# A mixing phase whose early stage is split in two, with new task orders, four banks for the streams' states, block tables built across partitions, and residual rows kept in SBUF

## The reference, cut to what matters

```python
h = rmsnorm(x, ln1)
proj = h @ w_in                                   # 3080 columns
out_a = rglru(conv(proj[:512])) * gelu(proj[512:1024])
q, k, v = silu(conv(proj[1024:2560]));  z, beta, g = ...
# gated DeltaNet, 4 heads of 128: a scan over blocks of tokens
L = strict_lower(kb @ k.T * decay);  T = inv(I + L)
v_new = T @ (v*beta) - (T @ (kb*exp(gc))) @ S
o = (q*exp(gc)) @ S + (q @ k.T * decay) @ v_new
S = S*exp(g_last) + (k*exp(g_last-gc)).T @ v_new  # one S per head, per stream
x2 = x + concat(out_a, rmsnorm(o)*silu(z)) @ w_out
h2 = rmsnorm(x2, ln2)
grp, top-2 experts of the group, weights = router(h2)      # 32 experts
y[expert, slot] = (silu(h2 @ w1[e]) * (h2 @ w3[e])) @ w2[e]
out = rmsnorm(x2 + w_a*y[a] + w_b*y[b], final_g)
```

## Time and profile before

| | us |
|---|---|
| time, median of 3 runs (4146.07 to 4170.18) | 4149.03 |
| time of the profiled execution | 4149.71 |
| span of that execution in its profile | 4148.0 |
| PE busy, share of the span | 3463.8, 84% |
| DVE busy | 1822.0, 44% |
| ACT busy | 1314.6, 32% |
| POOL busy | 812.7, 20% |

### The profile page before, as it was taken

How to read it: one execution, slowest core, us unless ns; L and a number is a source line. 1 busy time by engine, 2 the same in 40 slices (tenths; PEclk the granted TensorE clock), 3 DMA queues, 4 the chain that set the end, 5 groups by cost and what they waited for, 6 DMA issues and landing times. The chain is left out here.

```text
span 4148.0 us, 60697 instructions
## 1 busy us (share of the span) xinstructions
PE 3463.8 (84%) x17484; PEld 2069.8 (50%) x17485; DVE 1822.0 (44%) x4823; ACT 1314.6 (32%) x2593; POOL 812.7 (20%) x1018
## 2 busy tenths in 40 slices
PE   7999999999975688888888877739999999999910
PEld 3444444444455666666666655624444444444400
DVE  6555456445544456556555555441111111111157
ACT  6455445545451233333323323201111111111122
POOL 0000000000001334434343433211111111111145
PEclk9999999999986799999999989859999999999965
DMA  4311111111013443443434333123445555553279
GB/s 144 102 49 48 51 66 38 53 51 53 33 39 123 131 121 116 127 120 114 130 99 129 96 98 103 50 108 143 182 182 200 186 187 207 197 188 121 86 309 379
DMA packets 334866, 514.03 MB, mean 124 GB/s; under 512 B 79874, under 2 KB 228834, under 8 KB 325986
## 3 DMA queue, kind: packets, MB, share of 16 engines
q1 hardware_dynamic: 251538, 279.19, 21.2%
q10 hardware_dynamic: 54288, 146.56, 9.0%
q0 software_dynamic: 28864, 86.09, 5.9%
HBM read 341.49 MB, written 170.26 MB: 123 GB/s over the span
## 5 line engine op out<-in xcount | busy, mean ns | idle before, releaser
L1745 PE MATMUL ebank<-w,rowsT 128*128 x1568 | 699.9, 600 | 32.6 <-SPq L1695 29.3
L298 PE MATMUL pP<-h_hi,w_hi 128*128 128x512 f16 (+1 forms) x1728 | 624.3, 365 | 31.4 <-DVE h_lo L480 16.8
L298 PE MATMUL pP<-h_lo,w_hi 128*128 128x512 f16 (+1 forms) x1728 | 624.3, 365 | 0.0
L298 PE MATMUL pP<-h_hi,w_lo 128*128 128x512 f16 (+1 forms) x1728 | 624.1, 365 | 0.0
L1745 PEld LDWEIGHTS ebank<-w,rowsT 128*128 128x128 f32 x1568 | 299.8, 192 | 418.5 <-issue 418.5
L1763 PE MATMUL ebank<-w,guT 128*128 x784 | 353.4, 593 | 2.6 <-ACT guT L1784 2.6
L1812 DVE TENSOR_TENSOR gu<-ebank,sil 128x256 f32<-128x256 f32 x98 | 41.6, 425 | 692.5 <-ACT sil L1780 692.5
L511 DVE SCALAR_TENSOR_TENSOR cv<-win,cols_sb,cv 128x512 f32<-128x512 f32 (+1 forms) x432 | 305.4, 707 | 35.1 <-issue 3.6
L1780 ACT ACTIVATE sil<-ebank 128x256 f32<-128x256 f32 x98 | 37.7, 385 | 814.8 <-PE ebank L1745 814.8
L298 PEld LDWEIGHTS pP<-h_hi,w_hi 128*128 128x128 f16 x1728 | 172.1, 100 | 220.6 <-issue 30.6
L298 PEld LDWEIGHTS pP<-h_lo,w_hi 128*128 128x128 f16 x1728 | 172.1, 100 | 187.2 <-issue 12.8
(11 more groups left out here) (308 smaller groups left out, 6237.1 us busy)
## 6 DMA issues: line engine op xcount, KB each, us to landing
w<-in_w SPq DMA_DIRECT2D x32, 2048.0 KB, 8.9
y<-yb ACTq DMA_DIRECT2D x98, 512.0 KB
ft<-mixin SPq DMA_DIRECT2D x33, 1280.0 KB, 7.1
mixin<-qo ACTq DMA_DIRECT2D x128, 256.0 KB, 2.0
w<-in_w SPq DMA_DIRECT2D x32, 1024.0 KB, 12.1
xt<-in_x SPq DMA_DIRECT2D x33, 512.0 KB, 5.1
kz<-mixin SPq DMA_DIRECT2D x33, 512.0 KB, 6.8
xr<-in_x SPq DMA_DIRECT2D x33, 512.0 KB, 5.3
```

Of the source, the lines that this page charges most:

```text
L298: ins = nc.tensor.matmul(pP[n % NPB][:, 0:N], w[:, k, c0:c0 + P], h[:, k, 0:N], start=(k + i == 0), stop=(k == KD - 1 and i == 2))
L1745: ins = nc.tensor.matmul((M0, M1)[p][:, :], xT[p][:, k, :], w13[:, bass.ds(s, 1), k * 512:(k + 1) * 512].rearrange("p a n -> p (a n)"), st ...
```

## The change

- **Mixing's early stage** becomes two: E (`gt`, `sq`, `stat`, `sse`, `ex`, `rr`, `fsc`) works on tile i+9, F (`gs`, `dec`, `DT`, `KK`, `G`, `QK`, `AT`, `ATm`) on i+8. In the prologue `stat` writes to bank YE, later to FB behind the previous tile's `QK`. `stat` computes 32 columns in a product and not 128. `sq` is ScalarE's first task of an iteration.
- **Task orders** are new on every engine: `x2` before `X`; `xn` before `vd`; GpSimd does `r2` right behind `eT`. The scatter is a stage Q one iteration later, in three pieces: `sct0` first of all, `sct1` behind `rr`, the wait for landing (`scd`) last.
- **SyncE** issues `early_load` between the stores of G and of AT, for a tile two ahead, so that it is there one iteration before its `sq`.
- **w_out** is split piece by piece, one in each of the first eight iterations. Setup waits for constants move to their first users.
- **The streams' states** use four banks and four mask buffers; ScalarE makes the masks.
- **Routing** is no phase of its own: the tables are computed with the blocks on partitions at the end of mixing (32 elements per operation), and turned into rows by two products on TensorE; the destinations are computed in three pieces at the start of the experts' phase, where the first weights are now loaded too.
- **Residual rows**: in the experts' phase SyncE also loads x2 of 28 tiles into SBUF (112 KB per partition), one after each expert's weights; the other five are loaded at the start of combining. Combining has no load of its own per tile any more.

```diff
 MIX = """
-Y.KS.pe Y.QS.pe Y.X.dve R.x2.dve Y.o1.act R.st.act X.eT.pool X.B16.pool X.eZ.pool R.r2.pool
-X.kt.pe X.vt.pe X.sc.dve X.ktc.act F.gs.dve F.sq.act
-Y.N.pe Y.vd.dve Y.vh.act X.vs.act R.xn.dve
-F.stat.pe F.sse.dve F.ex.act F.rr.pool X.B32.pool
-Y.dS.pe Y.AV.pe Y.S.dve
-R.hT0.pe R.hT1.pe R.hc0.dve R.hc1.dve Y.o.dve R.h2.pool
-X.W16.pe X.I16.dve F.dec.pe F.DT.act
-R.lg.pe F.fsc.dve R.r0.dve Y.so.act Y.ro.pool
-X.T16.pe X.T16c.act F.KK.pe F.G.dve X.B64.pool
-Y.outA0.pe X.Z16.pe X.Z16c.act R.r1.dve R.sh.act R.rx.act
+Q.sct0.pool X.eT.pool E.sq.act R.x2.dve Y.KS.pe Y.QS.pe Y.X.dve R.st.act Y.o1.act R.r2.pool X.B16.pool X.eZ.pool
+X.kt.pe X.vt.pe X.sc.dve E.gt.dve F.gs.dve X.ktc.act R.xn.dve
+Y.N.pe Y.vd.dve Y.vh.act X.vs.act
+E.stat.pe E.sse.dve E.ex.act E.rr.pool Q.sct1.pool R.h2.pool
+Y.dS.pe Y.AV.pe Y.o.dve Y.so.act Y.ro.pool
+R.hT0.pe R.hT1.pe R.hc0.dve R.hc1.dve
+X.W16.pe X.I16.dve Y.S.dve F.dec.pe F.DT.act E.fsc.dve
+R.lg.pe R.r0.dve X.T16.pe X.T16c.act X.B32.pool R.r1.dve
+F.KK.pe F.G.dve X.B64.pool
+Y.outA0.pe X.Z16.pe X.Z16c.act R.sh.act R.rx.act
 X.W32.pe X.I32.dve Y.outA1.pe Y.on.dve
-X.T32.pe X.T32c.act F.QK.pe F.AT.dve Y.oT.pe F.ATm.pool
+X.T32.pe X.T32c.act F.QK.pe F.AT.dve Y.oT.pe F.ATm.pool Q.scd.pool
...
-Y.outB0.pe Y.outB1.pe R.rk.pe V.v.dve R.off.dve R.sct.pool
+Y.outB0.pe Y.outB1.pe R.rk.pe V.v.dve R.off.dve
...
-                tiles_ = {st: tile_at(i, four, n) for st, n in (("F", LEAD), ("X", 1), ("Y", 0), ("R", -1))}
+                tiles_ = {st: tile_at(i, four, n) for st, n in (("E", LEAD + 1), ("F", LEAD), ("X", 1), ("Y", 0), ("R", -1), ("Q", -2))}
...
+                if after_first and four is None and 0 <= i + LEAD + 1 < KD:
+                    after_first(i + LEAD + 1)
...
                 if f is not None:
-                    early_store(f[0])
+                    G_store(f[0])
+                    if nf is not None:
+                        early_load(nf[0], nf[1])
+                    AT_store(f[0])
...
                 if n == "stat":
-                    pe.wait_ge(*at("AT", t, 1))
+                    if prologue(t):
+                        pe.wait_ge(*at("sse", t, 1))
+                        pe.wait_ge(*at("ex", t, 1))
+                    else:
+                        pe.wait_ge(*at("AT", t, 2))
+                    bank = flat(YE if prologue(t) else FB)
                     pe.wait_ge(*at("sq", t))
                     for c in range(2 * H):
-                        nc.tensor.matmul(flat(FB)[:, c:c + P], sqb[:, c, :], mat("ones"), start=True, stop=True)
+                        nc.tensor.matmul(bank[:, c:c + SW], sqb[:, c, :], mat("ones")[:, 0:SW], start=True, stop=True)
...
                 elif n == "dec":
-                    pe.wait_ge(*at("sse", t))
-                    pe.wait_ge(*at("ex", t))
+                    if stream or prologue(t + 1):
+                        pe.wait_ge(*at("AT", t, 1))
+                    else:
+                        pe.wait_ge(*at("sse", t, -1))
+                        pe.wait_ge(*at("ex", t, -1))
+                    pe.wait_ge(*at("gs", t))
...
                         for b in range(SB):
                             pe.wait_ge(vm_ready, b + 1)
+                            if b >= 4:
+                                pe.wait_ge(stream_S, b - 3)
                             for h in range(H):
-                                ins = nc.tensor.matmul(YC[:, h, :], ktok[p][:, h, :], vm[:, h, :], start=True, stop=True)
+                                ins = nc.tensor.matmul(turn_bank[b % 4][:, h, :], ktok[p][:, h, :], turn_vm[b % 4][:, h, :],
+                                                       start=True, stop=True)
                             ins.then_inc(stream_mm, 1)
-                            pe.wait_ge(stream_S, b + 1)
...
+            def routing():
+                v, part = nc.vector, col("part")
...
+                v.tensor_tensor_scan(end[:, :], start[:, :], nb[:, :], 0.0, ALU.mult, ALU.add)
+                v.tensor_scalar(past[:, :], end[:, :], part, None, ALU.is_le)
...
+                v.reduce_sum(route[:, 0:1], past[:, :], AX.X)
...
+                v.tensor_tensor(route[:, 1:2], route[:, 1:2], valid[:, :], ALU.mult).then_inc(route_columns, 1)
+                v.tensor_copy(tabs["end"][:, :], end[0:1, :])
+                dve.wait_ge(route_rows, 1)
+                v.tensor_copy(tabs["expert"][:, :], flat(YA)[0:1, 0:NB])
...
+            for p in range(2):
+                load_expert(sp, T, weights, p, p)
...
                     load_expert(sp, T, weights, pair * 2 + (2 + p), p)
+                    if keep:
+                        sp.dma_start(kept[0][:, bass.ds(pair * 2 + p, 1), :].rearrange("p a n -> p (a n)"),
+                                     T["x2"][bass.ts(pair * 2 + p, P), :]).then_inc(kept[1], 16)
...
+            def destinations():
+                iota, n = cols[:, COLS["iota"][0]:COLS["iota"][1]], 22
+                hot = yb[0][:, 0:n * NE].rearrange("p (t e) -> p t e", e=NE)
+                for c in range(0, 2 * NT, n):
...
+            destinations()
             program("dve", dve, step)
...
-                sp.dma_start(xx[p][:, :], T["x2"][bass.ts(t, P), :]).then_inc(x_in[p], 16)
+            for t in range(KEPT, NT):
+                sp.dma_start(late[:, t - KEPT, :], T["x2"][bass.ts(t, P), :]).then_inc(late_in, 16)
```

More of the change, by code:

```diff
@@ L37 @@
 FE = 256
+KEPT = NE - 4
 EPS = 1e-6
@@ L702, in mix_phase @@
         tid = sb("tid", [P, 1], I32)
+        cnt = sb("cnt", [P, NE], I32)
+        nb = sb("nb", [P, NE])
+        end = sb("end", [P, NE])
+        past = sb("past", [P, NE])
+        valid = sb("valid", [P, 1])
+        before = sb("before", [P, 1])
+        route = sb("route", [P, 2])
         FB, XA, XB, YA, YB, YC, YD, YE = [
@@ L761, in mix_phase, with prologue @@
         last = NT - 1
-        first_loop = 1
+        first_loop = 2
         loops = (last - 1 - LEAD - first_loop + 1) // BATCH
+        def prologue(t):
+            return isinstance(t, int) and t < LEAD
         def every(engine, iteration):
-            for i in range(-LEAD, first_loop):
+            for i in range(-LEAD - 1, first_loop):
                 iteration(i, None)
@@ L1281, in f_step @@
                     ins.then_inc(*did(n))
+                elif n == "gs":
+                    dve.wait_ge(*at("dec", t, 1))
+                    for h in range(H):
+                        ins = nc.vector.tensor_scalar(gs[:, h, :], mat("after_s" if stream else "after"),
+                                                      gt[p][:, H + h:H + h + 1], None, ALU.mult)
+                    ins.then_inc(*did(n))
                 elif n == "sse":
@@ L1634, in experts_phase @@
-def experts_phase(nc, T, const, tabs, weights):
+def experts_phase(nc, T, const, cols, eid, rank, start, dest, tabs, weights, kept):
     NT, NB = tiles(), blocks()
@@ L1836, in combine_phase @@
         yr = [[sb(f"yr{s}_{k}", [P, D]) for k in range(2)] for s in range(NR)]
-        xx = [sb(f"xx{s}", [P, D]) for s in range(NR)]
+        late = sb("late", [P, NT - KEPT, D])
         yo = [sb(f"yo{s}", [P, D]) for s in range(NS)]
@@ L1847, in combine_phase @@
         eps_set = sem("eps_set")
-        x_in = [sem(f"x2_in{s}") for s in range(NR)]
+        late_in = sem("late_in")
         y_in = [sem(f"y_in{s}") for s in range(NR)]
@@ L1992, in follow, with ahead @@
                 out(t, p)
-            with dve.Fori(0, NT // NR - 1) as four:
+            def ahead(t, p):
+                dve.wait_ge(y_in[p], both_fetched(t, p))
+                rows(t + NR, p)
+                follow(t, p)
+            whole = KEPT // NR - 1
+            with dve.Fori(0, whole) as four:
                 for p in range(NR):
-                    dve.wait_ge(y_in[p], both_fetched(four * NR + p, p))
-                    rows(four * NR + NR + p, p)
-                    follow(four * NR + p, p)
+                    ahead(four * NR + p, p)
+            for t in range(whole * NR, NT - NR - 1):
+                ahead(t, t % NR)
             rows(NT - 1, 0)
```

297 lines of the change are left out of this document (139 added, 158 removed).

## The result

The changed kernel takes 4057.05 us (median; the kernel before beside it 4158.74): a ratio of 0.9754, 95% interval 0.9709 to 0.9798. The forecast was 3902, the range began at 3855 and ended at 3985: the sign was right, the size was not. The medians differ by 101.7 us.

What follows compares the result with a forecast made beforehand. TensorE was taken to bound the experts, and a chain starting with GpSimd's queue the prompt tiles. Tiles 180, prologue 18, states 16, routing 25, residual rows 0 and combining 8 sum to 247 off 4149.7: 3902 us, range 3855 to 3985.

Steps and rivals of the forecast that it cites:

- Squares first: Prompt tiles: squares of q and k one tile ahead end TensorE's wait for them; 65 us gained, bounds 45 and 65.
- Scatter behind, `r2` forward: Prompt tiles: GpSimd's earlier `r2` brings `xn` early; 80 us back, 10 paid at `dS`, net 70, bounds 35 and 90.
- Narrow products: Full prompt tiles: passes with 32 columns instead of 128 start closer together; 25 us gained, bounds 0 and 32.
- Clock: Prompt tiles: with idle stretches gone, TensorE's granted clock partly comes back; 20 us gained, bounds 0 and 40.
- Prologue: Start of mixing: with E a tile ahead the scalars leave the chain between G's; 18 us gained, bounds 0 and 30.
- Streams' states: Eight state updates: with four banks the longest step decides; 14 us off plus 2, together 16, bounds 10 and 20.
- Routing: Between mixing and experts: tables hidden inside GpSimd's scatter wait, first expert product earlier; 25 us gained, bounds 18 and 28.
- Residual rows: Experts' phase: the 28 extra loads behind each expert's weights cost nothing; 0 us, bounds 0 and -6.
- combining: Combining: with a quarter fewer bytes, DVE's 4.65 us binds all 32 distances; 8 us gained, bounds 4 and 12.
- the stages hardly overlap more: Rival, prompt tiles: a chain through `vd` and `dS` replaces T's wait, clock stays 0.95; 3982; 0.28 with the VectorE rival.
- The one on VectorE: Rival, prompt tiles: DVE becomes the bound, 36.5 us a tile and not 33.9; 3985; 0.28 with the overlap rival.
- The one that was to end slower: Rival, full tiles: q and k load late and block ScalarE, 4200 us and more; chance 0.03.

Runs made afterwards that it cites:

- experiment 11: Changed kernel with `vd` ahead of `xn` on VectorE, but GpSimd's old order (both scatters, T, B16, Z, then `r2`): 4067.86 us, ratio 0.9789 to the kernel before.
- experiment 1: Changed kernel with `vd` ahead of `xn` in VectorE's task order: 4004.55 us, ratio 0.9625 to the kernel before.
- experiment 4: Changed kernel with the squares' and gates' products 128 columns wide again instead of 32: 4031.4 us, ratio 0.9694 to the kernel before.
- experiment 5: Kernel before the change with only the squares' and gates' products cut from 128 to 32 columns: 4195.71 us, ratio 1.0085 to the kernel before.
- experiment 6: Changed kernel with, in the prologue alone, the load of the tile two ahead issued before G's nine stores: 4045.92 us, ratio 0.9738 to the kernel before.
- experiment 7: Changed kernel with 128-column squares' products and a task order of its own for the prologue: 4022.28 us, ratio 0.9662 to the kernel before.
- experiment 3: Changed kernel with stage F ahead of stage E on every engine in the prologue: 4046.9 us, ratio 0.9729 to the kernel before.
- experiment 10: Changed kernel with `vd` ahead of `xn`, 128-column squares' products, the prologue's own order, and `xn` on ScalarE behind `vh`: 3964.82 us, ratio 0.9521 to the kernel before.

## Why the prediction was right and wrong

The time came out above the range because two steps failed, in the tiles (84.7 us for 180) and in the prologue (-36.7 for +18). In the tiles the step that failed is the overlap at the norm: `vd` behind `xn` was to cost `dS` 10 us and cost 62 more than before. In the prologue it is the path: the scalars did not leave the chain, and G's came 20.7 us apart for the 10.5 forecast. Two terms had the wrong sign besides, the narrow products and, in the full tiles, the clock.

*Squares first.* The wait went as forecast, 64.9 us to nothing. The time did not: the 25 tiles that have squares got 42.0 us shorter by all the edits together, so part of what was saved here was paid again at `dS` and in the clock. In the prologue the same step turned into the wait of 7.7 us a tile ahead of L952.

*Scatter behind, `r2` forward: net 70, bounds 35 and 90.* The step named its own risk, "`vd` stands behind `xn` on DVE now and `dS` waits for it", and priced it at 10 us; it cost 62. Two links in front of `xn` were laid out wrongly: T was given its blocks at once (it waited 73.8 us for them, SyncE's load coming after G's stores and five other transfers), and `xn` the 0.76 us that it took when GpSimd was quiet (1.75 here). The first half, GpSimd's order, is worth 63 us by experiment 11. The second, VectorE's, costs 53 by experiment 1. The second ate most of the first; what was left of 70 shows in the seven tiles without squares (42.7 us) and hardly in the full ones.

*Narrow products: 25, bounds 0 and 32.* The row was misread. The 0.07 us a pass of the earlier trace rows is the distance of starts within four passes that follow a product of 512 columns. The weight loads of the same four passes, in the same stretch of the kernel before, tell more:

```profile
1936.70 0.41 PEld L1089 LDWEIGHTS bank<-OO,const 128*128 128x128 f32 x2
1937.03 0.30 PEld L1090 LDWEIGHTS bank<-OO,const 128*128 128x128 f32 x2
1937.17 0.18 PEld L1069 LDWEIGHTS bank<-w_out_hi,mx_hi 128*128 128x128 f16 x1
```

The four loads take 0.47 us until the next one starts, 0.117 each: the first began beside the long product ahead, and that alone let the passes come closer. Sixteen in a row have nothing to hide behind and take just this, 0.117 with 32 columns, and 0.122 with 128 (experiment 4). The Trainium skill, "TensorE: Matmul & The Clock Gate", section "Back-to-back issue gap", adds that weight loads raise the distance above its floor; that was the half of its rule to go by, and for these passes it left next to nothing. (By that floor the term would be 57 us, as an estimate, 22 passes of 0.103 us less in 25 tiles, and not some 50.) The low bound said it, "weight loads could bind", and a bound below zero was missing: by the clock the edit costs 25 us in the changed kernel (ratio 0.9754 against 0.9694, experiment 4) and 35 to 39 in the one before (experiment 5).

*Clock: 20.* It went the other way in the full tiles, 0.95 to 0.93 (TensorE busy 7.5 us longer), and in the prologue, 0.66 to 0.53; in the seven tiles without stage F it came back as forecast, 0.88 to 0.95 (8.4 us less). What was argued, that less idle time brings it back, holds there and by experiment 1 (0.96; 1.00 in the tiles without stage F). In the full tiles of the changed kernel the wait at `dS` kept it down, 0.95 even with wide products (experiment 4), and the narrow products took the rest.

*Prologue: 18, bounds 0 and 30.* The failed step is "with E a tile ahead in its own bank the scalars leave the chain". They did not, because an order within each engine's queue, not a bank, holds them: `stat` of the tile ahead stands before `dec`, and it waits for a load that is issued behind nine stores. That is the low bound's own word, "SP's nine stores", with no price below zero. Of the 36.7 us 2.3 are the later start of mixing, and 4.2 the extra iteration, forecast 4 (from the first load to the first G 23.9 us against 19.7, with G's first start at 1275.07 and 1268.52). The other 30.2 are the loop from the first G to the first KS: 9.4 of them by the clock (gone in experiment 4), the rest by its order (experiments 6 and 7). Experiments 3 and 7 show what the sum left out besides: once `stat` is out of the way, `gs` stands on VectorE behind the w_out piece and the inversion's half, which were priced as work and not as links. And `dec` at full clock, as in the earlier trace rows (1.13 us), is not "at the low level, which holds here": that level held in part of the prologue.

*Streams' states: 16.* Right, 20.0. Updates now follow each other on VectorE without a gap, 32 in one row:

```profile
2635.41 8.36 DVE L1442 SCALAR_TENSOR_TENSOR S_s<-S_s,exS,bank 128x128 f32<-128x128 f32 x32 [2.13 <-PE bank L1069]
```

*Routing: 25, bounds 18 and 28.* 15.3. The tables are hidden behind the scatter as laid out; the first up-product then waits for the list and the gather one after the other (26.5 us of idle TensorE before the first transposes), which the sum had at 12 us from the end of mixing and which take 22. They now run beside two experts' weights on the same DMA engines; before, the weights were loaded under VectorE's tables. GpSimd's gather behind its wait for the list, before and after:

```profile
2791.20 1.02 POOL L1716 DMA_INDIRECT rows<-h,idx  x1 [2.57 <-DMA idx<-table]
```

```profile
2702.89 1.01 POOL L1728 DMA_INDIRECT rows<-h,idx  x1 [7.19 <-DMA idx<-table]
```

From there to the first transposes it took 4.6 us before and 9.6 after. Together the list and the gather take 9.7 us longer beside the weights, and 9.7 is what the term lacks. No run moved the weights, so the cause is read from these two traces alone.

*Residual rows: 0, bounds 0 and -6; combining: 8.* Right within the bounds, 3.6 lost and 8.5 gained; the sums of two tiles are 4.61 us apart (the second sums, 3902.9 to 4050.5 in 32 steps), forecast 4.65.

Of the rivals, "the stages hardly overlap more" came nearest: its chain through `vd` and `dS` is the one found, and the clock did not rise (0.93 over the 32 tiles). It was put at 3982 because it was summed with a prologue that gains 18. The one on VectorE had the other half of the mechanism, `xn` and `vd` in a row beside GpSimd's B16, and 36.5 us a tile (36.8 measured); but it is the order on VectorE and not its load, 24.3 us of 38.1 in a full tile, since swapping two tasks took the wait away (experiment 1). The one that was to end slower named the late load of q and k, but in the full tiles, where it is harmless; in the prologue, where the same load closes a loop, it was not looked for.

What stays open: why full tiles stay at 36.2 to 36.6 us where TensorE has 32 us of work. The largest waits left are WI and `lg`, then KS and the load of `ft`, and experiment 10 says only that 1.9 us less work on VectorE does not end them. Open too is why the narrower products lower the clock.

## What to carry to other kernels

When a producer is moved forward on an in-order queue, price what it now stands in front of: `xn` was early at last, and its own wait became that of everything behind it. When a task is moved to one tile ahead, walk once round the loop in the stretch where nothing else covers it; a load issued behind the stores of the stage that it feeds is a link of that loop. And the price of fewer columns is to be read from the starts of the weight loads as well as of the passes, over as many passes in a row as the edit has, together with the granted clock of the stretch.

## What the runs showed that was not expected

- Products of the squares and gates with a quarter of the columns, same count and same order, lower the granted clock: 0.66 to 0.53 in the prologue and 0.95 to 0.89 in the full tiles of the kernel before (35 to 39 us), 0.69 against 0.53 and 0.95 against 0.93 in the kernel after (25 us). They save 0.08 us a tile themselves. With `vd` first, at clock 0.96, the width makes 4.7 us in the full tiles.
- A VectorE instruction of 0.75 us takes 1.75 beside a GpSimd product of 1.25 us, and 0.94 beside GpSimd products of 0.45 us.
